# A diffusion step with a grouped mixture of experts, one core: one weight load moved ahead of two others, the routing of three token tiles taken apart and its order rewritten

## The reference

```python
D_MODEL = 1024; BATCH = 1; SEQ = 128; DEC_BATCH = 1; DEC_SEQ = 512
N_EXPERTS = 16; N_EXPERT_GROUPS = 4; EXPERTS_PER_GROUP = 4; TOP_K = 2; D_FF = 512; N_MOD = 6

def _layer(x, mod, rope, ctx, p):
    shift1, scale1, gate1, shift2, scale2, gate2 = jnp.split(mod[:, None, :], N_MOD, axis=-1)
    h = _rms(x, p['norm1_g']) * (1.0 + scale1) + shift1
    ...                                   # three branches: retention, attention, S5
    merged = (jax.nn.sigmoid(g_ret) * ret_branch + jax.nn.sigmoid(g_att) * att_branch
              + jax.nn.sigmoid(g_ssm) * ssm_branch)
    x = x + gate1 * (merged @ p['w_out'])
    h2 = _rms(x, p['norm2_g']) * (1.0 + scale2) + shift2
    x = x + gate2 * _moe(h2, ...)

def _moe(h, w_router, b_router, w_gate, w_up, w_down):
    logits = (h @ w_router).astype(jnp.float32) + b_router.astype(jnp.float32)
    probs = jax.nn.softmax(logits, axis=-1)
    grouped = probs.reshape(b, n, N_EXPERT_GROUPS, EXPERTS_PER_GROUP)
    group_score = jnp.sum(lax.top_k(grouped, TOP_K)[0], axis=-1)
    best = jnp.argmax(group_score, axis=-1)
    in_group = jnp.arange(N_EXPERT_GROUPS) == best[..., None]
    masked = jnp.where(in_group[..., None], grouped, -1.0).reshape(b, n, N_EXPERTS)
    top_v, top_i = lax.top_k(masked, TOP_K)
    ...                                   # weights of the two experts
    hid = jax.nn.silu(jnp.einsum('bld,edf->blef', h, w_gate)) * jnp.einsum('bld,edf->blef', h, w_up)
    return jnp.einsum('blef,efd->bld', hid * combine[..., None], w_down)
```

## Time and profile before

| what | us |
|---|---|
| median of 3 runs | 1310.59 |
| lowest and highest run | 1306.53, 1310.75 |
| the profiled execution, its own time | 1310.76 |
| its span in the trace | 1309.0 |
| PE busy in it | 1202.4 (92%) |
| DVE busy | 546.6 (42%) |
| ACT, POOL busy | 211.8 (16%), 219.4 (17%) |

### The profile page before, as it was taken

One profiled execution on the slowest core, in us unless ns is written; L12 is line 12 of the kernel. 1 busy time (PEld: TensorE's weight loads), 2 busy tenths in 40 slices (PEclk: granted clock), 3 DMA queues, 4 the chain that ended last, 5 costly groups with the idle time before them and its releaser, 6 DMA issues. The chain is left out here.

```text
span 1309.0 us, 15039 instructions
## 1 busy us (share of the span) xinstructions
PE 1202.4 (92%) x5900; PEld 585.1 (45%) x5900; DVE 546.6 (42%) x1245; ACT 211.8 (16%) x527; POOL 219.4 (17%) x329
## 2 busy tenths in 40 slices
PE   3799999999988999999999999899798998999993
PEld 1445555454856544444444444345453333333331
DVE  2687546839445313333312223324673221121237
ACT  2111112203353222222210100101100000000001
POOL 3008400010079330000000122320120000000030
PEclk9799999999999999999999999999788998999997
DMA  9421601140320171101202565662179999999982
GB/s 302 181 69 58 106 28 58 65 62 4 120 61 21 65 295 58 65 14 51 65 19 110 209 193 201 240 240 88 43 260 360 387 384 361 382 375 381 392 309 97
DMA packets 96190, 221.86 MB, mean 169 GB/s; under 512 B 9384, under 2 KB 11304, under 8 KB 95600
## 3 DMA queue, kind: packets, MB, share of 16 engines
q1 hardware_dynamic: 80256, 173.52, 37.0%
q0 software_dynamic: 14128, 41.01, 10.3%
q10 hardware_dynamic: 1728, 6.29, 1.2%
HBM read 190.32 MB, written 28.38 MB: 167 GB/s over the span
## 5 line engine op out<-in xcount | busy, mean ns | idle before, releaser
L837 PE MATMUL banks<-wring,HT 128*128 128x512 f32 x480 | 216.4, 598 | 0.0
L664 PE MATMUL banks<-wring,HT 128*128 128x512 f32 (+1 forms) x480 | 196.1, 569 | 0.5 <-ACT REG L1361 0.5
L1074 PE MATMUL banks<-REG 128*32 128x512 f32 x1008 | 178.0, 596 | 1.5 <-DMA REG<-w_gate 1.5
L970 PE MATMUL banks<-wring,REG 128*128 128x512 f32 x320 | 139.4, 594 | 1.5 <-DVEq L433 1.5
L664 PEld LDWEIGHTS banks<-wring,HT 128*128 128x128 f32 x480 | 92.0, 194 | 98.4 <-issue 95.3
L837 PEld LDWEIGHTS banks<-wring,HT 128*128 128x128 f32 x480 | 87.9, 191 | 95.6 <-issue 93.2
L970 PEld LDWEIGHTS banks<-wring,REG 128*128 128x128 f32 x320 | 60.1, 190 | 78.2 <-issue 76.2
L1074 PE MATMUL banks<-wring,REG 128*32 128x512 f32 x432 | 81.8, 632 | 2.6 <-DMA REG<-w_gate 2.6
L1074 PEld LDWEIGHTS banks<-REG 128*32 128x32 f32 x1008 | 47.3, 110 | 68.7 <-issue 66.9
L992 PE MATMUL banks<-wring,REG 128*128 128x512 f32 x160 | 72.7, 613 | 5.6 <-DMA wring<-w_out 5.6
L2000 DVE TENSOR_REDUCE REG<-banks 128x1 f32<-128x640 f32 (+1 forms) x40 | 26.8, 712 | 72.5 <-PE banks L911 72.5
(11 more groups left out here) (404 smaller groups left out, 1461.3 us busy)
## 6 DMA issues: line engine op xcount, KB each, us to landing
wring<-w_in SPq DMA_DIRECT2D x12, 2048.0 KB, 7.8
REG<-w_down SPq DMA_DIRECT2D x10, 2048.0 KB, 18.0
REG<-w_gate SPq DMA_DIRECT2D x9, 2048.0 KB, 22.5
HT<-w_ada SPq DMA_DIRECT2D x8, 2048.0 KB, 8.2
REG<-w_up SPq DMA_DIRECT2D x8, 2048.0 KB, 19.5
wring<-w_up SPq DMA_DIRECT2D x7, 2048.0 KB, 15.9
scratch_x<-REG POOLq DMA_DIRECT2D x17, 512.0 KB, 10.4
wring<-w_gate SPq DMA_DIRECT2D x4, 2048.0 KB, 17.5
```

Of the source, the lines that this page charges most:

```text
L664: last = mm(out[:, 0:cols], HT[:, k, P * t:P * t + P], w[:, k, 0:cols], start=k == 0, stop=k == KD - 1)
L837: last = mm(chan.bank(), HT[:, k, P * (i % NT):P * (i % NT) + P], gate[1][:, k, :], start=k == 0, stop=k == KD - 1)
L970: last = mm(out, x[:, k, P * t:P * t + P], w[:, k, :], start=k == 0, stop=k == 3)
L1074: last = mm(out[js, :], columns(k)[:, js], ws[j == 3][:, k, cols], start=k == 0, stop=k == ks - 1)
```

## The change

SP loads the first half of `w_out` earlier: behind the third-last `w_ada` block and in front of the last two `w_ada` blocks. The second half keeps its place.

In the routing, `choose` becomes three functions, `choose_group`, `choose_first` and `choose_second`, with the same instructions. For part 0 they no longer stand in a row: `residual(4, 0)`, `columns_in(3)`, `residual(4, 1)`, `logits(3)` and `normed(4)` stand between them, and `places(0)` follows `choose_second(0)`. `normed` of tile 4 works in two halves of 512 columns, the upper one first, and each half raises `h2_ready`. PE transposes each half of tile 4 when it is there. ACT evicts both halves of tile 4; the DVE copy `columns_in(4)` goes away. The two clearing matmuls of `pick(0)` become a step of their own (`clear`) ahead of `turn(4)`; the zeroed tile is written by DVE in front of `choose_group(0)`, and the wait for `bc_in` 64 moves there. On PE `logits(3)` now comes ahead of `rank(0)`, and `rank(0)` behind `turn(4)`. POOL's store of tile 4 waits for both halves.

```diff
--- before.py
+++ after.py
     OUT_STEPS = (("out", 0, 0), ("out", 1, 0), ("out", 0, 1), ("out", 1, 1), ("out", 2, 0), ("turn", 0), ("out", 2, 1), ("logits", 0),
                  ("turn", 1), ("out", 3, 0), ("logits", 1), ("turn", 2), ("out", 3, 1), ("logits", 2), ("out", 4, 0), ("turn", 3),
-                 ("out", 4, 1), ("rank", 0), ("logits", 3), ("turn", 4), ("logits", 4), ("pick", 0), ("rank", 1), ("pick", 1))
+                 ("out", 4, 1), ("logits", 3), ("clear",), ("turn", 4), ("rank", 0), ("logits", 4), ("pick", 0), ("rank", 1), ("pick", 1))
...
         def turn_rows(t):
-            pe.wait_ge(h2_ready, t + 1)
             for half in (1, 0):
-                transposes((vec, sca)[half == 1], [NROWS[:, t, P * k:P * k + P] for k in range(4 * half, 4 * half + 4)])
+                pe.wait_ge(h2_ready, t + 1 + (t == NT - 1 and half == 0))
+                transposes((vec, sca)[half == 1 or t == NT - 1], [NROWS[:, t, P * k:P * k + P] for k in range(4 * half, 4 * half + 4)])
             turned[t] = vec.k, sca.k
...
         def pick(part):
 
             lo, hi = ROUTE_PARTS[part]
-            pe.wait_ge(picked, part + 1)
-            if part == 0:
-                for half in range(2):
-                    mm(banks[:, 6 + half, :], PICK[:, NT - 1, :], NROWS[:, 0, 0:512], start=True, stop=False)
+            pe.wait_ge(picked, part + 2)
             for t in range(lo, hi):
                 for k in range(KD):
                     last = mm(banks[:, 6 + k // 4, P * (k % 4):P * (k % 4) + P], NROWS[:, t, P * k:P * k + P], PICK[:, t, :],
...
+        def clear():
+
+            pe.wait_ge(picked, 1)
+            for half in range(2):
+                mm(banks[:, 6 + half, :], PICK[:, NT - 1, :], NROWS[:, 0, 0:512], start=True, stop=False)
+
+        steps = dict(out=project_out, turn=turn_rows, logits=logits, rank=rank, pick=pick, clear=clear)
...
+        loaded_ahead = []
+
+        def load_block(ahead=None):
+            n = n_loaded[0] if ahead is None else ahead
+            if ahead is None:
+                n_loaded[0] += 1
+                if n in loaded_ahead:
+                    return
+            else:
+                loaded_ahead.append(n)
             w, rows, c0, cols = blocks[n]
             if slot_before[n] is not None:
                 sp.wait_ge(*released[slot_before[n]])
...
+        while n_loaded[0] < FIRST_LAST_BLOCK - 2:
+            load_block()
+        load_block(FIRST_LAST_BLOCK)
         while n_loaded[0] < FIRST_LAST_BLOCK:
             load_block()
         sp.wait_ge(gates_used, 5)
...
         def columns_in(t):
-            src = sca.take(act)
-            sca.give(A(LCOLS[:, t % 2, 4:8, :], src.rearrange("p (a b) -> p a b", a=4), ACT.Copy))
+            for half in (1, 0) if t == NT - 1 else (1,):
+                src = sca.take(act)
+                sca.give(A(LCOLS[:, t % 2, 4 * half:4 * half + 4, :], src.rearrange("p (a b) -> p a b", a=4), ACT.Copy))
...
                 dve.wait_ge(bc_in, 48)
-            done(stt(h, X2[:, t, :], y, BCSC[:, s, :], ALU.mult, ALU.mult))
-            tt(h, h, BCSH[:, s, :], ALU.add).then_inc(h2_ready, 1)
+            for cols in (slice(512, D), slice(0, 512)) if t == NT - 1 else (slice(0, D),):
+                done(stt(h[:, cols], X2[:, t, cols], y, BCSC[:, s, cols], ALU.mult, ALU.mult))
+                tt(h[:, cols], h[:, cols], BCSH[:, s, cols], ALU.add).then_inc(h2_ready, 1)
...
-        def choose(part):
+        def first_largest(part, onehot, value, x, m, tmp):
+
+            lo, hi = ROUTE_PARTS[part]
+            n, largest = hi - lo, ROUTE[:, 1, lo:hi]
+            over = lambda x, m: x.unsqueeze(2).broadcast_to([P, n, m])
+            red(value, x, ALU.max)
+            done(tt(tmp, x, over(value, m), ALU.is_equal))
+            done(tt(tmp, tmp, DESC[:, 0:m].unsqueeze(1).broadcast_to([P, n, m]), ALU.mult))
+            red(largest, tmp, ALU.max)
+            done(tt(onehot, tmp, over(largest, m), ALU.is_equal))
+
+        def choose_group(part):
 
...
+            first_largest(part, gh[7], c(0), gh[4], NG, gh[0])
             done(ts(gh[7], gh[7], 2.0, -2.0, ALU.mult, ALU.add))
             done(tt(p4, p4, gh[7].unsqueeze(3).broadcast_to([P, n, NG, EG]), ALU.add))
-            first_largest(m1, c(2), prob, NE, eq)
+
+        def choose_first(part):
+
+            lo, hi = ROUTE_PARTS[part]
+            prob, eq, m1 = (x[:, lo:hi] for x in (PROB, EQ, M1))
+            first_largest(part, m1, ROUTE[:, 2, lo:hi], prob, NE, eq)
             done(stt(flat2(prob), flat2(m1), -3.0, flat2(prob), ALU.mult, ALU.add))
-            first_largest(m2, c(3), prob, NE, eq)
+
+        def choose_second(part):
+
+            lo, hi = ROUTE_PARTS[part]
+            prob, eq, m1, m2, mb = (x[:, lo:hi] for x in (PROB, EQ, M1, M2, MB))
+            first_largest(part, m2, ROUTE[:, 3, lo:hi], prob, NE, eq)
             done(tt(mb, m1, m2, ALU.add))
...
-            dve.wait_ge(bc_in, 64)
             for t in range(lo, hi):
                 going(ts(PICK[:, t, :], PLACES, RANK[:, t, 0:1], MB[:, t, 0:1], ALU.is_equal, ALU.mult))
-            if part == 0:
-                going(V_.memset(PICK[:, NT - 1, :], 0.0))
             dve.wait_ge(dve_step, steps_so_far())
             dve.sem_inc(picked, 1)
...
         residual(3, 1)
         normed(3)
         logits(2)
-        choose(0)
+        dve.wait_ge(bc_in, 64)
+        V_.memset(PICK[:, NT - 1, :], 0.0).then_inc(picked, 1)
+        choose_group(0)
         residual(4, 0)
         columns_in(3)
+        choose_first(0)
         residual(4, 1)
+        logits(3)
         normed(4)
+        choose_second(0)
         places(0)
-        logits(3)
-        columns_in(4)
         logits(4)
-        choose(1)
+        choose_group(1)
+        choose_first(1)
+        choose_second(1)
+        dve.wait_ge(picked, 1)
         places(1)
...
         def stored(t):
-            pool.wait_ge(h2_ready, t + 1)
+            pool.wait_ge(h2_ready, t + 1 + (t == NT - 1))
             pool.dma_start(scratch_h2[P * t:P * t + P, :], NROWS[:, t, :]).then_inc(h2_out, 16)
```

More of the change, by code:

```diff
@@ L1038, in pick @@
                 last.then_inc(row_t, 1)
-        steps = dict(out=project_out, turn=turn_rows, logits=logits, rank=rank, pick=pick)
+        def clear():
[3 more added lines that the diff above has]
+        steps = dict(out=project_out, turn=turn_rows, logits=logits, rank=rank, pick=pick, clear=clear)
         for step in OUT_STEPS:
@@ L1187, in _ @@
         n_loaded = [0]
-        def load_block():
-            n = n_loaded[0]
-            n_loaded[0] += 1
+        loaded_ahead = []
[7 more added lines that the diff above has]
+                loaded_ahead.append(n)
             w, rows, c0, cols = blocks[n]
@@ L2112, in choose @@
             over = lambda x, m: x.unsqueeze(2).broadcast_to([P, n, m])
-            logit, prob, eq, m1, m2, mb = (x[:, lo:hi] for x in (LOGIT, PROB, EQ, M1, M2, MB))
+            logit, prob = (x[:, lo:hi] for x in (LOGIT, PROB))
             gh = [x[:, lo:hi] for x in GH]
@@ L2127, in choose @@
             done(tt(gh[4], gh[4], gh[5], ALU.add))
-            def first_largest(onehot, value, x, m, tmp):
-                red(value, x, ALU.max)
-                done(tt(tmp, x, over(value, m), ALU.is_equal))
-                done(tt(tmp, tmp, DESC[:, 0:m].unsqueeze(1).broadcast_to([P, n, m]), ALU.mult))
-                red(c(1), tmp, ALU.max)
-                done(tt(onehot, tmp, over(c(1), m), ALU.is_equal))
-            first_largest(gh[7], c(0), gh[4], NG, gh[0])
+            first_largest(part, gh[7], c(0), gh[4], NG, gh[0])
             done(ts(gh[7], gh[7], 2.0, -2.0, ALU.mult, ALU.add))
             done(tt(p4, p4, gh[7].unsqueeze(3).broadcast_to([P, n, NG, EG]), ALU.add))
-            first_largest(m1, c(2), prob, NE, eq)
+        def choose_first(part):
+            lo, hi = ROUTE_PARTS[part]
+            prob, eq, m1 = (x[:, lo:hi] for x in (PROB, EQ, M1))
+            first_largest(part, m1, ROUTE[:, 2, lo:hi], prob, NE, eq)
             done(stt(flat2(prob), flat2(m1), -3.0, flat2(prob), ALU.mult, ALU.add))
-            first_largest(m2, c(3), prob, NE, eq)
+        def choose_second(part):
+            lo, hi = ROUTE_PARTS[part]
+            prob, eq, m1, m2, mb = (x[:, lo:hi] for x in (PROB, EQ, M1, M2, MB))
+            first_largest(part, m2, ROUTE[:, 3, lo:hi], prob, NE, eq)
             done(tt(mb, m1, m2, ALU.add))
```

## The result

The changed kernel takes 1295.72 us in the median (1294.43 to 1300.88, 4 runs), the kernel before, run beside it, 1309.92. The ratio is 0.9892 with a 95% interval of 0.987 to 0.9914. The profiled execution took 1296.46 us, with a span 14.3 us shorter than that of before.

What follows compares the result with a forecast made beforehand. PE, busy 92% of the span, was taken as the bound, except where DVE's routing chain and the rows' way start the expert stage. 8.6 + 4.6 = 13.2 off 1310.76, less 0.17 for the median, gave 1297.4 us; range 1293 to 1302.

Steps and rivals of the forecast that it cites:

- The forecast case: Whole kernel: the start and the routing both gain as reckoned, 10 to 14 us; chance 0.75.
- its sign: Whole kernel: faster by more than the 3.9 us that a measurement can tell from no change; chance 0.92.
- The front, 8.6 us: First output projection: the earlier `w_out` load removes 5.6 us of waiting and 3.0 us of low clock.
- the clock's share, 3.0 us: First projection tile: without a pause ahead of it, it runs at the full clock level, saving 3.0 us.
- the rival in which they share: SP's loads at the start: `w_out` and `w_ada` share evenly, PE waits at 814; 1303 us, chance 0.05.
- DVE's chain to the end of the choosing, 21.5 us from the last projection tile: Routing: DVE ends choosing for part 1 at 953.5 in old trace times, the last projection tile ending at 932.00.
- `pick(0)`, 5.52 us: Routing on PE: runs at the full level without its clearing pair and ends at 952.1, before the ranks.
- The rival for this case: Routing: low clock makes `pick(0)` take 11 us, leaving 0.5 of the 4.6 gain; about 1301.5 us, chance 0.12.
- The split of tile 4: Routing, normalisation in two halves: costs 0.5 us, brings the first half 1.0 us ahead of an unsplit tile.
- Given back: Expert stage: scatter or weights limited by something not moving with the routing; 1307 to 1311 us, chance 0.05.
- slower by the expert stage's clock: Expert stage: longer or more broken pauses keep PE at 1.2 GHz, 34 us more at low level; 1315 us, chance 0.03.
- The sum: Whole kernel: 8.6 at the start plus 4.6 in the routing, 13.2 us off one execution.

Runs made afterwards that it cites:

- e8b: Kernel before, with six 512-column matmuls that nobody reads put into PE's wait for the first half of `w_out`; 1306.99 us.
- e3: Changed kernel with the first `w_out` load one place further ahead on SP, in front of the third-last `w_ada` load; 1296.33 us, one run.
- e5: Changed kernel with the choosing of part 0 in one piece again, before tile 4's residuals; 1298.06 us.
- e7: Changed kernel with tile 4 normalised in one piece of 1024 columns again; 1295.52 us.
- e9: e7 with four extra matmuls that nobody reads ahead of the clearing pair; 1297.46 us.
- e4: Changed kernel with four extra 512-column matmuls that nobody reads ahead of the clearing pair; 1295.82 us.
- e8_fill: Kernel before, with 13 matmul calls that nobody reads put into PE's wait for `w_out`; 1312.57 us, median of nine runs.

## Why the prediction was right, and where it was not

1297.4 us was forecast and 1295.72 measured. That is inside the range of 1293 to 1302, in the part that the forecast allowed for scatter, below its own 1296.6 to 1300.6. The forecast case and its sign were right; one term, `pick(0)`, was wrong, and that the total came so near is in part luck (see the sum).

- **The front, 8.6 us.** Right in each part: 8.7 in the trace. The wait is gone, and the clock's share, 3.0 us, was measured by itself at 2.8 in e8b. The second half of `w_out` landed 10.0 us after its issue at 840.61, 8 us ahead of the tile that wants it. The loads on SP queue up (e3), so the rival in which they share is ruled out. By the Trainium skill (DMA: Bandwidth & Descriptors, Queues, rings and completion order) descriptors are consumed in ring order on each DMA engine, but a later one may finish its write before an earlier one. The runs agree with the first and don't show the second for whole loads: in none of the 13 traces does a weight load on SP land before the one issued ahead of it.
- **DVE's chain to the end of the choosing, 21.5 us from the last projection tile.** Right: 21.6 (944.07 - 922.44). Taking the choosing of part 0 apart is worth 1.5 us of it (e5).
- **`pick(0)`, 5.52 us.** This is the term that failed. It was taken at the full level and took 8.00. It ends 22.4 us behind the projection instead of the 20.1 forecast, holds the ranks for 0.6 us, and with 0.1 more in the choosing and 0.1 in the ranks makes 23.3 us out of 22.5. The routing gained 3.8 instead of 4.6. The reason given for the full level was that PE is busy without a pause from the ranks of part 0 on. That held, from 932.55, but the level stayed low until 941.9, through 9.3 us of work without a gap. The case that the forecast went by, the first projection tile of before, had the full level back 5.8 us after its start (851.13 to 856.9). In the four traces of the changed routing `pick(0)` took 7.55 to 8.38 us, so the miss is no accident of one trace, while what it cost differs: the ranks were held 0.1 to 1.0 us. The rival for this case had the right mechanism and too high a price, as the clock came back in the middle of `pick(0)`, not behind it. What the forecast watched for, a `pick(0)` of over 7 us with `rank(1)` right behind it, is what the trace shows.
- **The split of tile 4.** The price of 0.5 us was right in kind: 930.35 - 927.48 = 2.87 for the four instructions in after, against 2.46 for the two. What it was to buy, the first half 1.0 us ahead, is worth nothing, because the ranks of part 0, which stand ahead of tile 4's logits on PE, wait for `choose_second(0)` behind it on DVE. Without the split the choosing of part 1 ends 0.3 us earlier (e7). The forecast saw this wait and did not draw the conclusion.
- **Given back, or slower by the expert stage's clock.** Neither came. The rows keep their distance of 26.1 us from `places(1)`. PE's wait for them grew to 5.23 us, and the low level ends a like time behind the start of the rows in both kernels: at 993.4 in before (8.2 us on) and at 979.4 in after (7.6 us on). The Trainium skill (TensorE: Matmul & The Clock Gate, HAM oscillation) describes a kernel whose clock falls at every wait between bursts of matmuls. The trace of after agrees for the wait ahead of the rows and for the pause ahead of tile 4's transposes, but not for every wait: over the 2.10 us ahead of PE's two units the clock stayed at 1.00. The fall inside a busy `pick(0)` in e9 is not of that kind either.
- **The sum.** 13.2 us were forecast for one execution, and 14.3 measured in its span. The parts of the change gave 12.5. The other 1.7 are 0.8 ahead of the front and 0.9 behind the rows, where nothing was changed. From the rows to the end it was 322.4 to 326.4 us over all runs of this study, so that last part is within what executions differ by. What the routing fell short by, 0.8, was thus more than made up by places that the change doesn't touch, and that is luck. For the 1.7 us by which the median lies under the forecast no cause is shown. One possibility: the forecast took the old routing from the execution of before, whose 27.1 us to `places(1)` is the lowest of four traces.

## What to carry to other kernels

A wait of the bounding engine can have the price of its clock besides its length (5.6 us and 2.8 us here); filling the wait with work that nobody reads measures that price by itself. When an order is rewritten so that two engines meet at one step, the length of every instruction group between them must be taken at the clock level that the rows beside it show, not at the level it had in its old surroundings. A split that brings a first half forward is worth something only if what the next engine waits for last is that half.

## What was not expected

- Keeping PE busy ahead of the routing did not keep its clock. Counted from the end of the last projection tile, it fell after 5.8 us in the changed kernel (8.2 in e3, with the same routing), after 9.8 in e4, and after 12.2 in e9 (at 935.3, and again at 945.5). In e4 it fell within the second of two short waits. In e9 it fell while PE was busy with no gap, 0.1 us into `pick(0)` and its 128-column matmuls, 2.4 us after the last wait. In e7, without the extra matmuls, it held through the whole pause of 4.14 us and fell 0.65 us after PE had begun again. What sets the moment of the fall stays open.
- The low level lasted very differently: 13.7 us in the changed kernel (928.2 to 941.9), 10.2 in e3 with the same routing, and 3.4 in e9's first fall (935.3 to 938.7).
- One call of a 512-column fp32 matmul is two instructions of 0.43 us in the trace, 0.86 to 0.87 us together at the full level, which is where the size of e8_fill went wrong by a factor of two.
